# Order of the work around the first chunk of the gated DeltaNet scan in a two-layer hybrid trunk

## The reference, cut to what matters

```python
q = l2norm(q) * GDN_DK ** -0.5
k = l2norm(k)
g = -exp(a_log) * softplus(a + dt_bias);  beta = sigmoid(b)
def gdn_chunked(q, k, v, g, beta, s0, want_out):
    cum = cumsum(g, axis=-1)                                # within a chunk
    decay = exp(where(incl, cum[..., :, None] - cum[..., None, :], -inf))
    kk = einsum('nbhid,nbhjd->nbhij', k, k)
    t_mat = where(strict, beta[..., :, None] * kk * decay, 0.0) + eye(c)
    sol = triangular_solve(t_mat, rhs, lower=True, unit_diagonal=True)
    ...
    v_new = uc - wc @ s
    s_next = s * g_last + k_tail.T @ v_new
    o = q_dec @ s + (qk * decay) @ v_new
```

## Time and profile before

| what | before |
|---|---|
| median of three runs | 2773.3 us |
| lowest, highest | 2768.41, 2779.13 us |
| profiled execution, its own time | 2770.12 us |
| its span, first to last instruction | 2768.3 us |
| PE busy | 2633.3 us (95%) |
| PE weight loads busy | 2251.4 us (81%) |
| DVE busy | 1549.1 us (56%) |
| ACT busy | 951.5 us (34%) |
| POOL busy | 561.8 us (20%) |
| chain that ended last, by engine | PE 81%, DVE 10%, ACT 4%, DMA 3%, issue 2% |

### The profile page before, as it was taken

One profiled execution on the slowest core, in us unless ns is written; L12 is line 12 of the kernel. 1 busy time (PEld: TensorE's weight loads), 2 busy tenths in 40 slices (PEclk: granted clock), 3 DMA queues, 4 the chain that ended last, 5 costly groups with the idle time before them and its releaser, 6 DMA issues.

```text
span 2768.3 us, 49905 instructions
## 1 busy us (share of the span) xinstructions
PE 2633.3 (95%) x21190; PEld 2251.4 (81%) x21190; DVE 1549.1 (56%) x2714; ACT 951.5 (34%) x1502; POOL 561.8 (20%) x232
## 2 busy tenths in 40 slices
PE   7899999999999999999999989899999999999998
PEld 1399888999999999997897538788778787888776
DVE  5745777527753443434637654678648653352656
ACT  0335333322323343224432234443333323332542
POOL 0122000120123212321123512200131232242032
PEclk8999999999999999999999999999999999999999
DMA  7421000333222113220134651100143321331033
GB/s 250 168 70 45 19 27 30 111 114 109 76 92 82 63 44 113 79 84 30 40 118 152 205 182 69 47 26 26 58 164 120 109 99 50 100 121 66 30 122 114
DMA packets 95164, 250.95 MB, mean 91 GB/s; under 512 B 11010, under 2 KB 32516, under 8 KB 94432
## 3 DMA queue, kind: packets, MB, share of 16 engines
q1 hardware_dynamic: 84170, 219.56, 23.4%
q10 hardware_dynamic: 10774, 28.19, 2.9%
HBM read 205.12 MB, written 35.26 MB: 87 GB/s over the span
## 4 chain that ended last, share of the span: by engine, by line
PE 81%; DVE 10%; ACT 4%; DMA 3%; issue 2%; SPq 0%; ACTq 0%; DVEq 0%
PE ps L1005 18%; PE ps L1007 17%; PE ps L1006 17%; PE ps L1013 6%; PE ps L1625 4%; PE ps L1022 3%; PE ps L1034 2%; PE ps L1145 2%; PE ps L1652 2%; PE ps L1635 2%; PE ps L1649 2%; DVE t_gcv L2346 1%; PE ps L1191 1%; PE ps L1099 1%; DMA t_raw<-in_w_ada 1%
## 5 line engine op out<-in xcount | busy, mean ns | idle before, releaser
L966 POOL TENSOR_TENSOR t_wlo<-t_raw,t_whi 128x1024 fp32r<-128x1024 f32 x217 | 535.1, 2467 | 2133.4 <-ACT t_whi L1758 2133.4
L1005 PE MATMUL ps<-t_u_hi,t_whi 128*128 128x384 f32 (+1 forms) x2368 | 848.0, 358 | 18.7 <-ACT t_oT L1829 6.7
L1007 PE MATMUL ps<-t_u_hi,t_wlo 128*128 128x384 f32 (+1 forms) x2368 | 826.8, 349 | 0.0
L1006 PE MATMUL ps<-t_u_lo,t_whi 128*128 128x384 f32 (+1 forms) x2368 | 826.2, 349 | 0.0
L1758 ACT ACTIVATE t_whi<-t_raw 128x1024 fp32r<-128x1024 f32 x235 | 248.5, 1057 | 791.9 <-PE ps L1007 679.8
L1005 PEld LDWEIGHTS ps<-t_u_hi,t_whi 128*128 128x128 f32 x2368 | 446.5, 189 | 54.5 <-issue 19.9
L1007 PEld LDWEIGHTS ps<-t_u_hi,t_wlo 128*128 128x128 f32 x2368 | 446.1, 188 | 23.8
L1006 PEld LDWEIGHTS ps<-t_u_lo,t_whi 128*128 128x128 f32 x2368 | 446.8, 189 | 21.3 <-issue 0.5
L1829 ACT ACTIVATE t_grp<-ps 128x256 f32<-128x256 f32 (+2 forms) x192 | 80.4, 434 | 229.3 <-PE ps L1022 132.7
L1005 PE MATMUL ps<-t_b_hi,t_whi 128*128 128x384 f32 (+1 forms) x384 | 137.6, 358 | 6.1 <-DVE t_acc L2338 3.4
L2346 DVE SCALAR_TENSOR_TENSOR t_gcv<-ps,t_par,t_gcv 128x128 f32<-128x128 f32 (+8 forms) x192 | 84.9, 495 | 102.6 <-ACT t_gcv L1829 100.8
(11 more groups left out here) (306 smaller groups left out, 3846.3 us busy)
## 6 DMA issues: line engine op xcount, KB each, us to landing
t_raw<-in_w_in SPq DMA_DIRECT2D x184, 512.0 KB, 3.6
t_raw<-in_w_ada SPq DMA_DIRECT2D x48, 512.0 KB, 4.4
t_raw<-in_w_br SPq DMA_DIRECT2D x32, 512.0 KB, 3.7
t_raw<-in_w_out SPq DMA_DIRECT2D x24, 512.0 KB, 3.8
t_sg<-gate_logits SPq DMA_DIRECT2D x28, 384.0 KB, 4.4
hs<-t_hstage ACTq DMA_DIRECT2D x20, 512.0 KB, 4.7
t_hring<-hs SPq DMA_DIRECT2D x20, 512.0 KB, 6.1
t_prob<-t_pT ACTq DMA_DIRECT2D x56, 128.0 KB, 2.1
```

What stands on the lines that cost most here:

```text
L966: pool.tensor_tensor(lo, raw[:, s % RAW, :], hi.bitcast(f32), ALU.subtract)\
L1005: pe.matmul(o, lh, rh, start=first, stop=False)
L1006: pe.matmul(o, lh, rl, start=False, stop=False)
L1007: return pe.matmul(o, ll, rh, start=False, stop=last)
```

## The change

The eight decay rows of DVE are formed at projection 8. PE's eight decay matmuls are issued right after the gate tiles, ahead of the last v transposes. On ACT the one-element exponential and the two decay exponentials stand ahead of the last v copy and the key copies (with a wait for its own last SiLU, since `grp` shares memory with the convolution's buffers). The keys are normalised by four instructions of 128 x 768, one for each head, and PE waits for each head alone. DVE, not ACT, copies heads 1 and 3 of the transposed keys (semaphore `k_t_dve`). In the first chunk DVE does `row_of`, `first_y`, `first_x` for direction 0 and then for direction 1.

```diff
--- before.py
+++ after.py
@@ -363,7 +363,7 @@
                  "f_mlp", "f_arg", "f_sin", "f_h4", "f_sd", "f_w4", "f_fo", "f_oc", "f_ev", "f_stage",
                  "ln_var", "ln_sd", "ln_n", "ln_x", "ln_t", "ln_u", "ln_split",
                  "cv_tap", "cv_done", "cv_silu", "q_sq", "q_sum", "q_sum_ok", "kv_t", "kv_tok",
-                 "k_sum", "k_sd", "k_norm", "k_t", "k_t_ok", "ab_w", "ab_ps", "ab_f", "ab_t", "ab_z", "ab_act", "ab_g",
+                 "k_sum", "k_sd", "k_norm", "k_t", "k_t_ok", "k_t_dve", "ab_w", "ab_ps", "ab_f", "ab_t", "ab_z", "ab_act", "ab_g",
                  "cum_ps", "cum_exp", 
                  "g_gm", "g_d", "g_ed", "g_kk", "g_qk", "g_m", "g_a", "g_c", "g_x0",
                  "g_q", "g_q_ok", "g_p", "g_pt", "g_x", "g_y", "g_yf", "g_ktail", "g_ks", "g_r", "g_vn", "g_vn_ok", "g_pre",
@@ -1273,12 +1273,23 @@
                         lend("cum_exp", 5)
                 for _ in range(first_tiles(l) * gate_units(l)):
                     next(gates)
+                for d in range(2):
+                    decay(0, d)
                 after(11)
-
-                pe.wait_ge(sems["k_norm"], l + 1)
                 for h in range(HEADS):
-                    spread(lambda t: ktok[:, t, h * P:(h + 1) * P], NT, 1 + h % 3, "k_t", "k_t_ok")
-                ln.take("k_t_ok", HEADS)
+                    ln.take("k_norm")
+                    spread(lambda t: ktok[:, t, h * P:(h + 1) * P], NT, 1 + h % 3, "k_t", "k_t_dve" if h % 2 else "k_t_ok")
+                ln.take("k_t_ok", HEADS // 2)
+                ln.take("k_t_dve", HEADS // 2)
+
+            def decay(t, d):
+                if t == NT:
+                    return
+                ln.take("g_gm")
+                claim(3 * d)
+                upto = cst[:, C_GE if d else C_LE, :]
+                ln.done(heads(3 * d, lambda h, c: from_row(t, d)[:, c], lambda h, c: upto), "g_d")
+                lend("g_ed", 3 * d)
 
             def gdn_scan(l):
                 freed["g_s"] = freed.get("g_s", 0) + 1
@@ -1290,15 +1301,6 @@
                 def tokens(t, d):
 
                     return slice(chunk(t, d) * P, (chunk(t, d) + 1) * P)
-
-                def decay(t, d):
-                    if t == NT:
-                        return
-                    ln.take("g_gm")
-                    claim(3 * d)
-                    upto = cst[:, C_GE if d else C_LE, :]
-                    ln.done(heads(3 * d, lambda h, c: from_row(t, d)[:, c], lambda h, c: upto), "g_d")
-                    lend("g_ed", 3 * d)
 
                 def k_by_k(t, d):
                     if t == NT:
@@ -1386,8 +1388,6 @@
                     ln.done(heads(6, lambda h, c: grp[:, d, 6, c], lambda h, c: grp[:, d, 0, c]), "g_oa")
                     lend("g_o2", 6)
 
-                for d in range(2):
-                    decay(0, d)
                 for d in range(2):
                     k_by_k(0, d)
                 for d in range(2):
@@ -1969,19 +1969,22 @@
                         ln.done(run(ssq[:, 3, :], ssq[:, 1, :], ACT.Sqrt, bias=eps), "k_sd")
                 for _ in range(2):
                     next(evacs)
+                run(bst[:, 0, 0, 0:1], eps, ACT.Exp)
+                ln.own("cv_silu")
+                for d in range(2):
+                    decay(0, d)
                 tok(11)
-                for h in range(HEADS):
-                    ln.take("k_t")
+                for h in range(0, HEADS, 2):
+                    act.wait_ge(sems["k_t"], HEADS * l + h + 1)
                     ln.done(run(kT[:, h, :], slot(1 + h % 3)[:, 0:TOK], ACT.Copy), "k_t_ok")
-                run(bst[:, 0, 0, 0:1], eps, ACT.Exp)
+
+            def decay(t, d):
+                if t == NT:
+                    return
+                ln.take("g_d")
+                ln.done(run(grp[:, d, 1, :], ps[:, 3 * d, :], ACT.Exp), "g_ed")
 
             def gdn_scan(l):
-                def decay(t, d):
-                    if t == NT:
-                        return
-                    ln.take("g_d")
-                    ln.done(run(grp[:, d, 1, :], ps[:, 3 * d, :], ACT.Exp), "g_ed")
-
                 def row_x(t, d, lv):
                     if t == NT:
                         return
@@ -2615,16 +2616,30 @@
                             step(ts(dirs(gsc[:, 3, :], d), dirs(ec[:, 2 * d, :], d), -1.0, None, ALU.mult))
                             step(tt(dirs(gsc[:, 2, :], d), dirs(ec[:, 2 * d + 1, :], d), dirs(gsc[:, 0, :], d), ALU.mult))
                         ln.step(dve.memset(state[:, :, :], 0.0), "g_s")
+                    if j == 8:
+                        for d in range(2):
+                            log_decays(0, d)
                     if j == 11:
                         dve.wait_ge(sems["k_sd"], l + 1)
                         step(dve.reciprocal(ssq[:, 2:4, :], ssq[:, 2:4, :]))
-                        ln.done(tt(kh, kh, ssq[:, 3, :].unsqueeze(2).broadcast_to([P, NT * HEADS, P]), ALU.mult),
-                                "k_norm")
+                        kt, r = ktok.rearrange("p i (h d) -> p i h d", h=HEADS), ssq[:, 3, :].rearrange("p (i h) -> p i h", h=HEADS)
+                        for h in range(HEADS):
+                            ln.done(tt(kt[:, :, h, :], kt[:, :, h, :], r[:, :, h].unsqueeze(2).broadcast_to([P, NT, P]),
+                                       ALU.mult), "k_norm")
+                for h in range(1, HEADS, 2):
+                    dve.wait_ge(sems["k_t"], HEADS * l + h + 1)
+                    ln.done(dve.tensor_copy(kT[:, h, :], slot(1 + h % 3)[:, 0:TOK]), "k_t_dve")
                 ln.due["kv_tok"] += 4
 
+            def log_decays(t, d):
+                if t == NT:
+                    return
+                i, m = chunk(t, d) * 8 + d * 4, cst[:, C_LT if d else C_GT, :]
+                for h in range(HEADS):
+                    last = ts(from_row(t, d)[:, h * P:(h + 1) * P], m, gs[:, 9, i + h:i + h + 1], None, ALU.mult)
+                ln.done(last, "g_gm")
+
             def gdn_scan(l):
-                g9 = gs[:, 9, :]
-
                 def wanted(t, d):
 
                     return 0 <= t < NT and (l == 0 or chunk(t, d) < LT)
@@ -2632,14 +2647,6 @@
                 def at(t, d):
 
                     return chunk(t, d) * 8 + d * 4
-
-                def log_decays(t, d):
-                    if t == NT:
-                        return
-                    i, m = at(t, d), cst[:, C_LT if d else C_GT, :]
-                    for h in range(HEADS):
-                        last = ts(from_row(t, d)[:, h * P:(h + 1) * P], m, g9[:, i + h:i + h + 1], None, ALU.mult)
-                    ln.done(last, "g_gm")
 
                 def each(f):
                     for h in range(HEADS):
@@ -2731,15 +2738,11 @@
                         ln.take("g_oa")
                         ln.step(tt(gtok[:, c, :], ps[:, 6, :], gtok[:, c, :], ALU.add), "g_o2")
 
-                for d in range(2):
-                    log_decays(0, d)
                 fence(ln, "dve")
                 step(dve.memset(grp[:, :, 4, :], 0.0))
                 for d in range(2):
                     row_of(0, d)
-                for d in range(2):
                     first_y(0, d)
-                for d in range(2):
                     first_x(0, d)
                 for t in range(NT):
                     log_decays(t + 1, 0)
```

## The result

Over 19 executions the changed kernel has a median of 2780.04 us (2774.57 to 2785.09), the kernel before 2773.69 us (2764.97 to 2779.13, also 19). The ratio is 1.0022, 95% interval 1.0013 to 1.0031: about 6 us slower, with an interval from 3.6 to 8.6 us. The prediction took 0.5% for the least that a measurement can tell from no change; with 19 executions of each kernel 0.22% is clear of zero. The median lies 0.04 us outside the range of 2766 to 2780. What has to be explained is that the kernel became slower where the forecast had no change. Three later executions, of 3210, 4313 and 6202 us, are left out of the ratios and of the table of all runs.

What follows compares the result with a forecast made beforehand. The prediction took TensorE (PE), busy 2633.3 us, as the bound. Layer 0's -0.5 us and layer 1's +0.45 summed to about 0, so the median stayed 2773.3 us, range 2766 to 2780.

Steps and rivals of the forecast that it cites:

- Decay rows at projection 8, no cost: DVE's eight decay rows, at most 3.76 us, fit its 5.13 us idle time at projection 8; no cost, no gain.
- Rival (a): Exponentials done before PE needs bank 3, so key transposes follow the v transposes: 5.4 us less, 2767.9 us; chance 0.1.
- ACT as what comes late next: ACT's table load and exponentials, 2.70 us, free bank 3 at 269.3 and 1782.2, delaying layer 0's key transposes 2.0 us.
- DVE's copy, 0.95 us taken: DVE's copy of a key head from PSUM takes 0.95 us, bounds 0.73 to 1.2, one on the path per layer.
- K by k 0.55 us earlier and 0.45 us later, sum zero: Start of k by k after the key copies: 0.55 us earlier in layer 0, 0.45 later in layer 1, together about 0.
- Direction 0 first, nothing: First chunk: direction 0's row product goes 2.5 us ahead, but PE's in-order queue waits for direction 1; gain nothing.
- rival (b): Early short product in the hole before the first row products keeps 2.4 GHz: up to 4.4 us less, 2768.9 us; chance 0.1.
- the landing of the key heads: Key transposes take PE 0.69 us a head; copied heads land at 270.3 to 272.3 and 1783.1 to 1785.2.
- rival (c): Idle PE before the key transposes drops to half clock: 3 us more, 2776.3 us, or 2779 with both layers; chance 0.3.
- The clock at 0.50 during the key transposes: Sign in the later profile that the forecast is wrong: PE at its 1.2 GHz level while transposing keys.
- a shift is carried on unchanged: After the first row products the instruction order is as before and PE is the bound, so any shift stays the same.
- the 0.02 for each side: Chance left for a time below or above the range of 2766 to 2780 us, for what was overlooked.

Runs made afterwards that it cites:

- e3: Changed kernel with PE's decay matmuls and ACT's one-element and decay exponentials moved back behind the key copies; 2771.98 us, ratio 0.9991 to the kernel before.
- e6: Changed kernel with unread filler matmuls: 8 and 14 (layers 0, 1) ahead of the key transposes, 7 ahead of each first row product; 2764.14 us, ratio 0.9964.
- e10: Changed kernel with 7 filler matmuls ahead of each first row product, none ahead of the key transposes; 2769.72 us, ratio 0.9985.
- e5: Kernel before with 13 filler matmuls ahead of the first row products of each layer; 2763.58 us, ratio 0.9967.
- e8: Changed kernel with the early decays moved back and DVE handling both directions in turn, as before the change; 2771.27 us, ratio 0.9986.
- e1: Kernel before with 26 filler matmuls ahead of the first row products of each layer; 2771.34 us, ratio 0.9992.
- e12: Kernel before, unaltered, run again for a second trace; 2770.08 us in its one execution.
- e4: Changed kernel with all four key copies on ACT again, none on DVE; 2778.11 us, ratio 1.0020 to the kernel before.

## Why the prediction was wrong, step by step

*Decay rows at projection 8, no cost.* Nothing speaks against it: e3 keeps them there and is not slower than the kernel before.

*Rival (a).* It did not come about: ACT released the key transposes in both layers.

*ACT as what comes late next.* Right, to a few tenths. Bank 3 was to be free at 269.3 and 1782.2. The key transposes started at 269.56 with all of layer 0 0.3 us later than before, and at 1787.02 with layer 1 4.6 us later, which is 1782.4. The table load and dummy exponential took what the earlier trace rows had. ACT's timeline of the changed kernel:

```profile
266.94 1.28 ACT L1829 ACT_TABLE_LOAD   x1
268.24 0.20 ACT L1829 ACTIVATE t_bst<-t_cst 128x1 f32<-128x1 f32 x1
268.35 1.07 ACT L1829 ACTIVATE t_grp<-ps 128x512 f32<-128x512 f32 x2
269.30 0.82 ACT L1829 ACTIVATE t_acc<-ps 128x768 f32<-128x768 f32 x1
```

The drain that the Trainium skill ("ScalarE: Activation LUTs", What ACT_TABLE_LOAD costs) counts on top of a load does not show here either: the next activation starts 1.30 us after the load's start, in the new place as in the old, and the load starts within 0.02 us of the end of what stood before it.

*DVE's copy, 0.95 us taken.* 0.96 us in each of four copies, for instance:

```profile
271.12 0.96 DVE L2631 COPY t_g_kT<-ps 128x768 f32<-128x768 f32 x1 [3.40 <-PE ps L1099]
```

*K by k 0.55 us earlier and 0.45 us later, sum zero.* Counted from the reciprocal of the norms, k by k starts after 10.67 and 13.52 us before, 11.19 and 15.36 after: 0.5 and 1.8 us later. With the clock held up (e6) it is 9.92 and 13.82: 0.75 earlier and 0.30 later, and layer 0 of e10, without a filler there, has 9.92 too. So the sum was right for a PE at full clock, and wrong for the PE that there was. e5 and e6, the kernels before and after with fillers, agree to 0.6 us in their medians, as the sum said, though each has an interval of some 4 us.

*Direction 0 first, nothing.* Right by e8 against e3. The early product stood alone with holes of 1.87 and 1.96 us around it, and the clock fell behind them all the same. The doubt of rival (b) was justified: with this order the clock did not stay up. It stayed low for 6.8 and 10.2 us in e3 and for 6.8 us in both layers of e8; one trace of each does not show whether the order makes the difference.

*The step that failed* is the landing of the key heads. The sum let PE take 0.69 us for each head ("PE's own pace holds it"), from 24 transposes in 2.84 us at full clock, although it had just put an idle stretch of 2.1 us (layer 0) and 3.2 us (layer 1) in front of them. They took 4.09 and 4.18 us, with the granted clock at 0.50 for part of them, and k by k came 1.1 and 1.4 us later than the sum had it (11.19 and 15.36 us after the reciprocal, against 10.12 and 13.96). I had named this as rival (c), with its mechanism, its place and the two rows between which it decides, 1.58 and 3.96 us of idle time. Then I gave it 0.3 and the forecast 0.5, although layer 1's hole of 3.2 us (3.69 measured) lay next to 3.96. Both layers fell, and both again in the second trace. "The clock at 0.50 during the key transposes" was one of the prediction's own signs of being wrong.

*A second step failed with it:* "a shift is carried on unchanged". K by k was 0.5 and 1.8 us late against the kernel before, but the first 64-column products were 2.3 and 0.9 us late (1.9 and 2.1 in the second pair of traces), and the whole kernel 6.

*Rival (c) came near by luck.* It priced 3 us a layer, 2779 us for both, 1 us below the measured median. But of its 2.3 us for the transposes only 1.3 were lost, as only part of them ran at 1.2 GHz. Its 0.7 us for k by k were not lost at all: that took 2.05 us as before. (Its rate is also off there: the eight products stand in the trace as 16 records.) The rest of the 6 us is elsewhere. Part of it is a longer fall at the first row products: 6.8 and 6.8 us, and 6.8 and 10.2 in the second trace, against 3.4 and 6.8 in both traces of the kernel before. The fall at the key transposes is not what makes it longer, as e3 has 6.8 and 10.2 us there without one. What makes it longer is not shown.

*The price of the clock was too low in rival (b) as well.* I bounded the gain of holding the clock by 4.4 us, half of the busy time in the two stretches of the earlier trace rows. The kernel before gave back about 10 us (4.7 to 13.9 by the interval) with fillers in just these two places. The bound rested on one trace, and a single trace holds one draw of something that differs from execution to execution: the kernel before varies from 2763 to 2783 us, and its time follows its clock.

*Slips that changed nothing.* The upper bound for DVE's copy, 0.84 us with a third again, is 1.1 us, not 1.2. The chances add up to 1 before the 0.02 for each side.

*What stays open.* Of the 10 us that fillers win in the kernel before, the trace of e5 shows only 3.2 us inside the two scans, counted from the reciprocal of the norms to the output norm (231.07 and 215.11 us, against 232.95 and 216.40). The two traced executions themselves are only 4.2 us apart; the rest is in executions that no trace shows. Also, the length of a hole is not all that decides. In e5 the clock fell in layer 0's key transposes, ahead of every filler and behind holes of only 1.58 and 0.61 us, just as they stand in the earlier trace rows, where it held. In e1 it fell there too, and the transposes took 4.50 us. The stretch of e5:

```profile
268.80:272.00 3.20, 3.20 (x17) 3.20 (x16) 2.91 (x8) 1.99 (x3) 1.46 (x1) 0.50 0.30 119
```

So with the old order this fall comes in some executions and not in others: it came in two of four traces of that passage (not in the kernel before and not in e12). What decides is not shown. After the change it came in both layers in all three traces with the early decays and no fillers (the changed kernel twice, and e4); e10, which has fillers only at the row products, fell there in layer 1 and not in layer 0.

## What to carry to other kernels

Before moving work so that TensorE waits longer at one place, look at the granted clock behind every existing hole of that length. Price the fall by experiment, not by half of the busy time in one trace: here 0.4 us were lost for each microsecond at 1.2 GHz. Where TensorE must wait for some microseconds in front of dense work, matmuls into an unused bank that end just before the wait does are a cheap edit to try. Count an fp32 matmul of 128 columns as two passes: overrunning the hole by 2 us ate most of the gain (e1 against e5). When executions of one kernel spread by 0.5%, compare their mean granted clocks before comparing their traces.

## What the hardware showed that was not expected

An fp32 matmul of 128 columns with fp32 operands stands in the trace as two matmuls of 0.11 to 0.12 us each at full clock (26 fillers: 52 records in 5.97 us).

Split by heads, the normalisation took 3.56 us in layer 0 against 3.36 in one piece, but 5.75 us in layer 1, off the path. There a split of the weights on POOL began before the last of the four. DVE's timeline, then POOL's:

```profile
1777.54 5.75 DVE L2339 TENSOR_TENSOR t_acc<-t_acc,t_ssq 128x768 f32<-128x768 f32 x4
```

```profile
1780.10 2.37 POOL L966 TENSOR_TENSOR t_wlo<-t_raw,t_whi 128x1024 fp32r<-128x1024 f32 x1 [5.39 <-ACT t_whi L1758]
```

The surplus of 2.2 us is about the length of POOL's instruction. This fits what the Trainium skill ("SBUF — State Buffer", Terms, on the shared port pair) says of a lock held for a whole instruction: the pieces of a split instruction can each be shut out by POOL, while one long instruction that is already running cannot. The kernel before looks the same way in layer 1: POOL's instruction that started under the long normalisation took 3.00 us instead of 2.37, and DVE's eight decay rows behind it took 5.85 us, against 3.76 in layer 0. No run was made for it.
